# Two activation functions, one table or two: how ScalarE is told which table to hold

## The reference

```python
for i in range(2):                       # first block; ctx is a second stream of 256 rows
    hx = rms_norm(x, g_mix[i]) * (1 + sc1) + sh1
    zx = hx @ w_in[i]                    # q, k, v, a pooling part, a Fourier part
    q = apply_rope(head_rms(zx_q, q_gain[i])); k = apply_rope(head_rms(zx_k, k_gain[i]))
    x = x + ga1 * (concat(attention, pool_mix, fourier_mix) @ w_out[i])
    fx = rms_norm(x, g_ffn[i]) * (1 + sc2) + sh2
    x = x + ga2 * swiglu(fx, w_gate_up[i], w_down[i])    # the same for ctx where i == 0
proj = modulate(x, norm1_g) @ w_in_2     # second block: attention, mLSTM, mixture of experts
attn = head_rms_norm(moba_attention(...)); hm = head_rms_norm(mlstm_chunkwise(...)) * sigmoid(o_m)
x = x + g1 * (concat(attn, hm) @ w_out_2)
x = x + g2 * hier_moe(modulate(x, norm2_g))              # 32 experts, every weight is read
return rms_norm(x, norm_f_g)
```

## Time and profile before

| what | value |
|---|---|
| time, median of 3 runs | 1589.12 us (1587.69 to 1589.77) |
| the profiled execution's own time | 1589.12 us |
| its span in the profile | 1587.3 us |
| TensorE busy | 1388.9 us, 88% |
| VectorE busy | 714.0 us, 45% |
| ScalarE busy | 500.9 us, 32% |
| GpSimd busy | 59.2 us, 4% |
| mean granted TensorE clock | 0.936 |
| read from HBM | 392.32 MB |

### The profile page before, as it was taken

How to read it: one execution, slowest core, us unless ns; L and a number is a source line. 1 busy time by engine, 2 the same in 40 slices (tenths; PEclk the granted TensorE clock), 3 DMA queues, 4 the chain that set the end, 5 groups by cost and what they waited for, 6 DMA issues and landing times.

```text
span 1587.3 us, 24627 instructions
## 1 busy us (share of the span) xinstructions
PE 1388.9 (88%) x10276; PEld 1042.8 (66%) x10276; DVE 714.0 (45%) x1306; ACT 500.9 (32%) x952; POOL 59.2 (4%) x52
## 2 busy tenths in 40 slices
PE   6999999999999999978999999999896677667564
PEld 3754576877778776847999989898653333333232
DVE  4446445555555564565655667676521111110101
ACT  3426424222122223454543444554310000000001
POOL 0100022000000012101000000000000000000000
PEclk8999999999999999999999999999997787887877
DMA  9637354645754563806456428245899999999996
GB/s 361 263 137 247 100 208 176 226 156 202 263 185 175 185 212 107 231 7 238 131 181 204 128 76 293 81 134 212 343 424 422 423 425 423 424 424 424 423 425 259
DMA packets 172651, 395.03 MB, mean 249 GB/s; under 512 B 11620, under 2 KB 124792, under 8 KB 150776
## 3 DMA queue, kind: packets, MB, share of 16 engines
q1 hardware_dynamic: 171816, 391.91, 66.4%
q10 hardware_dynamic: 720, 1.49, 0.2%
HBM read 392.32 MB, written 1.05 MB: 248 GB/s over the span
## 4 chain that ended last, share of the span: by engine, by line
PE 68%; DMA 22%; DVE 4%; ACT 3%; issue 2%; SPq 1%; POOL 0%; DVEq 0%; ACTq 0%; POOLq 0%
DMA R<-in_w_dram 20%; PE ps L985 15%; PE ps L986 15%; PE ps L991 15%; PE ps L2839 3%; PE ps L1007 2%; PE ps L1008 2%; PE ps L1013 2%; DMA R<-in_w_ada_dram 1%; PE ps L2888 1%; PE ps L1301 1%; PE ps L1358 1%; PE ps L2917 1%; PE ps L630 1%; PE ps L1332 1%
## 5 line engine op out<-in xcount | busy, mean ns | idle before, releaser
L954 DVE TENSOR_TENSOR WL<-R,WH 128x1024 fp32r<-128x1024 f32 (+1 forms) x202 | 225.3, 1128 | 140.1 <-ACT WH L944 140.0
L2839 PE MATMUL ps<-R,XG 128*32 128x256 f32 x2048 | 174.2, 501 | 119.2 <-DMA R<-in_w_dram 113.2
L985 PE MATMUL ps<-HH,WH 128*128 128x256 f32 (+2 forms) x872 | 274.3, 334 | 0.0
L986 PE MATMUL ps<-HL,WH 128*128 128x256 f32 (+2 forms) x872 | 270.8, 332 | 0.0
L944 ACT ACTIVATE WH<-R 128x1024 fp32r<-128x1024 f32 (+1 forms) x202 | 191.1, 961 | 156.3 <-PE ps L991 120.1
L2839 PEld LDWEIGHTS ps<-R,XG 128*32 128x32 f32 x2048 | 86.5, 138 | 200.7 <-issue 184.7
L985 PEld LDWEIGHTS ps<-HH,WH 128*128 128x128 f32 (+1 forms) x872 | 165.4, 190 | 24.6 <-issue 3.6
L986 PEld LDWEIGHTS ps<-HL,WH 128*128 128x128 f32 (+1 forms) x872 | 164.7, 189 | 16.3
L991 PE MATMUL ps<-HH,WL 128*128 128x256 f32 (+2 forms) x872 | 165.0, 331 | 0.0
L985 PE MATMUL ps<-GH,WH 128*128 128x512 f32 (+1 forms) x480 | 154.1, 340 | 0.0
L986 PE MATMUL ps<-GL,WH 128*128 128x512 f32 (+1 forms) x480 | 153.4, 338 | 0.0
(11 more groups left out here) (480 smaller groups left out, 1736.4 us busy)
## 6 DMA issues: line engine op xcount, KB each, us to landing
R<-in_w_dram SPq DMA_DIRECT2D x192, 1024.0 KB, 22.5
R<-in_w_ada_dram SPq DMA_DIRECT2D x72, 1024.0 KB, 6.9
R<-in_w_gate_up_dram SPq DMA_DIRECT2D x40, 1024.0 KB, 7.7
R<-in_w_in_dram SPq DMA_DIRECT2D x20, 1024.0 KB, 8.8
R<-in_w_down_dram SPq DMA_DIRECT2D x16, 768.0 KB, 4.5
R<-in_w_down_dram SPq DMA_DIRECT2D x16, 640.0 KB, 4.4
R<-in_w_in_dram SPq DMA_DIRECT2D x8, 512.0 KB, 7.2
R<-in_w_out_dram SPq DMA_DIRECT2D x16, 256.0 KB, 8.6
```

The source lines that it names most:

```text
L954: last = e.tensor_tensor(L, w, H.bitcast(F32), ALU.subtract)
L985: e.matmul(b[0:n, 0:N], H[:, k, 0:n], xh(k, N), start=(k == 0), stop=False)
L986: e.matmul(b[0:n, 0:N], H[:, k, 0:n], xl(k, N), start=False, stop=False)
L2839: mm = e.matmul(PS[4][32 * g:32 * g + 32, 0:256], x[:, 4 * hf + k, :], w[g // 2][:, k, 256 * (g % 2):256 * (g % 2) + 256], start=(hf == 0 ...
```

## The change

The requests for a table by name go away. In `act_rstd` a small activation of one column (`act_warm`: Ln of a constant, its result used by nobody) stands in their place, and in the second block two of the requests go with nothing in their place; the one for Sqrt becomes a one-column Sqrt. A new semaphore `s_warm` orders these small activations among themselves; its waits are for earlier instructions of the same engine.

```diff
-    LN_EXP = "natural_log_exp_and_others"
-
-    def act_rstd(e, n, N):
-        e.preload_act_table_set(LN_EXP)
+    def act_warm(e, w):
+
+        if w:
+            e.wait_ge(s_warm, w)
+        e.activation(EB[:, 1:2], ONES[:, 0:1], ACT.Ln).then_inc(s_warm, 1)
+
+    def act_rstd(e, n, N, w):
+        act_warm(e, w)
         e.wait_ge(s_sum, 8 + 3 * n)
...
         elif j == 25:
             act_silu2(e, 3)
-            e.preload_act_table_set(LN_EXP)
             act_head_squares(e, 0)
...
             e.activation(OM[:, :, :], OM[:, :, :], ACT.Sigmoid).then_inc(s_mla, 1)
-            e.preload_act_table_set(LN_EXP)
...
             if j == 3:
-                e.preload_act_table(ACT.Sqrt)
+                e.wait_ge(s_warm, 5)
+                e.activation(EB[:, 1:2], ONES[:, 0:1], ACT.Sqrt).then_inc(s_warm, 1)
```

More of the change, by code:

```diff
@@ L320, in block_program @@
     s_fd, s_fp, s_fq, s_r5, s_root = (sem(n) for n in ("s_fd", "s_fp", "s_fq", "s_r5", "s_root"))
-    s_cvt, s_wd = sem("s_cvt"), sem("s_wd")
+    s_cvt, s_warm, s_wd = sem("s_cvt"), sem("s_warm"), sem("s_wd")
     s_kq, s_hbc, s_hpk = sem("s_kq"), sem("s_hbc"), sem("s_hpk")
@@ L1737, in act_layer @@
             act_split(e, t0 + 1)
-            act_rstd(e, 2, 512)
+            act_rstd(e, 2, 512, 2)
         else:
@@ L1763, in act_layer @@
         act_split(e, t1 + 1)
-        act_rstd(e, 2 * i + 1, N)
+        act_rstd(e, 2 * i + 1, N, 2 * i + 1)
         act_norm(e, 2 * i + 1, N, i == 0, 256, lambda k: MOD[:, i, 24 + k, 0:1])
@@ L2383, in act_second @@
         e.dma_start(TWO[:, :], A["k_two"]).then_inc(d_two2, 16)
-        act_rstd(e, 4, 256)
+        act_rstd(e, 4, 256, 4)
         act_norm(e, 4, 256, False, 256, lambda k: MOD[:, 2, k, V2:V2 + 1])
@@ L3146, in _ @@
             act_square(e, 0, 5, 512)
-            act_rstd(e, 0, 512)
+            act_rstd(e, 0, 512, 0)
             act_layer(e, 0)
```

## The result

| | before | after |
|---|---|---|
| median of the runs shown together | 1588.51 us (1583.69 to 1589.77) | 1598.88 us (1597.83 to 1599.11) |
| ratio, 95% interval | | 1.0063 (1.0048 to 1.0079) |
| the profiled execution's own time | 1589.12 us | 1598.26 us |
| its span | 1587.3 us | 1596.5 us |
| ScalarE busy | 500.9 us | 523.5 us |

The changed kernel is slower by 0.63%. Between the two profiled executions it is 9.1 us, between the medians 10.4 us, and the interval of the ratio is 7.6 to 12.5 us. 1600.2 us had been forecast. The record has ten runs of the changed kernel, from 1594.14 to 1599.11 us with their median at 1598.35 us; the five of the table lie in the upper part of that.

What follows compares the result with a forecast made beforehand. TensorE was taken to bound the kernel up to about 1115 us, transfers from 1170 us on. The profiled 1589.12 us plus 9.38 of path and 1.7 of clock gave 1600.2 us, range 1595.5 to 1604.0 us.

Steps and rivals of the forecast that it cites:

- 9.38 us of path: Sum of forecast TensorE delays: norms 1 and 2, norms 3 and 4, layer 1 head norms, gates, last head norms.
- One load, 1.283 us and 0.02 us around it: On ScalarE, each added table load between close instructions costs 1.29 us; norms 1 and 2 together cost 2.58 us.
- The dearer switch: Rival: a load between Ln and Exp costs twice its length, 10.2 us more in all, 1610.4 us; chance 0.04.
- Norms 3 and 4, 2 x 1.49: At each of these norms, a one-column Ln of up to 0.20 us plus a load of 1.29 us; 2.98 us together.
- Head norms of layer 1, 1.26: Two loads each at keys and queries delay weight copies and VectorE's scaling, so TensorE's spreading of roots comes 1.26 us later.
- Gates, 1.28: A load before the gates' Ln delays a weight copy and the whole VectorE chain to the scores' exponential: 1.28 us.
- Last head norms, 1.28: Second block: two loads around the Ln delay rounding and scaling, so TensorE's transposes start 1.28 us later.
- The places at nothing: Norm 0, layer 0 head norms, first scores' Exp, second block's first head norms and the Sqrt: cost 0.
- The clock, +1.7: Longer TensorE stops at norms 1 and 2 bring a slow stretch behind at least one: +1.7 us, between 0 and +3.4.
- the likeliest case: Of none, one or two extra slow clock stretches (1598.5, 1600.2 or 1601.9 us), one was held likeliest.
- Not slower, because the experts' transfers take it in: Rival at 1113 to 1170 us: the weight stream starts independently of TensorE, so the end stays at 1589.1 us; chance 0.04.

Runs made afterwards that it cites:

- the kernel with the inner loads behind the waits: Kernel before plus the changed kernel's loads at layer 1 head norms (requested after the waits), gates and last head norms only: 1594.02 us, ratio 1.0045.
- the one with the loads costed at nothing: Kernel before plus eight loads at norm 0, layer 0 head norms, first scores' Exp and second block's first head norms: 1590.20 us, one run.

## Why the prediction was right

The forecast was 1600.2 us, the median 1598.9 us; 9.38 us of path had been summed, and the steps of the table, less the clock, are 9.0.

- **One load, 1.283 us and 0.02 us around it.** Right: 1.28 at norms 1 and 2 (1.29 forecast), and linear in the number of loads. The dearer switch is refuted, and with it, for this chip and this kernel, the drain of about 1380 ns that the Trainium skill adds in "ScalarE: Activation LUTs", section "What ACT_TABLE_LOAD costs"; its 1283 ns agree with all 34 loads. Where they differ the measurement decides.
- **Norms 3 and 4, 2 x 1.49.** The stops grew by 1.37 and 1.38. The one-column Ln had been put at up to 0.20, its busy time, and costs 0.10, the distance to the start of the Ln behind it: 0.2 us too much in the sum.
- **Head norms of layer 1, 1.26.** Right in size, 1.22, and nearly in its way: of this, 0.51 came behind the keys. There TensorE waited for the roots themselves, 0.43 us, and not for the copy behind them as I had it:

```profile
661.04 1.09 PE L1158 MATMUL ps<-RSK,HPK 32*128 32x512 f32 x2 [0.43 <-ACT RSK L1142]
...
670.64 0.36 PE L989 MATMUL ps<-HH,WH 128*128 128x256 f32 x1 [0.34 <-ACT WH L948]
```

- **Gates, 1.28.** Right: 1.27. The chain through VectorE has no slack.
- **Last head norms, 1.28.** The size was right, 1.22, the path was not: the place is TensorE's wait for the split at 1098.21, which this matmul did not have in before, and not the transposes, which I had delayed by the scaling of the heads:

```profile
1098.21 0.39 PE L1011 MATMUL ps<-M2H,WH 128*128 128x256 f32 x1 [1.17 <-DVE M2L L2085]
```

- **The places at nothing.** Right: no step at them that the kernel before doesn't show between its own two profiles.
- **The clock, +1.7.** The mechanism was right and its net size was not. One slow stretch did follow norm 1, and none norm 2, as the likeliest case had it. It cost 2.81 - 1.28 = 1.53 us. That it was one and not two is in part luck: stops of the same 2.89 us were followed by two in the kernel with one load in each norm. Norms 3 and 4 brought 0.06 and 0.49 more. But the profiled execution also came to norm 1 ahead of the one of before, by 1.66 us. The first matmul behind norm 0 was 0.71 us ahead already, here of before and then of the changed kernel:

```profile
37.78 0.79 PE L1007 MATMUL ps<-HH,WH 128*128 128x512 f32 x1 [2.81 <-DVE HL L829]
```

```profile
37.07 0.80 PE L1011 MATMUL ps<-HH,WH 128*128 128x512 f32 x1 [2.80 <-DVE HL L833]
```

Ahead of it TensorE had waited 2.1 us for the first weights in place of 3.0. The other 0.9 us came behind it, where the first slow time ended at 40.5 us in place of 43.1 (it was 10.2 us long where that of before was 13.7). Nothing shows that either comes from the change: the kernel with loads only in the experts' stage had 10.2 us of slow time there too, and the second profile of the changed kernel, with the same 10.2, came to norm 1 only 0.58 us ahead. So the profile shows the path's 9.0, the clock's +2.1 and the start's -1.7, and 9.35 in all; the medians show 10.4.

- **Not slower, because the experts' transfers take it in.** Refuted by the equal 460 us windows. The experiment in that stage shows how near it was: a delay of that size, and three times it, costs nothing when it falls behind the start of the stream.

The experts' stage began 9.45 us late, and I had written about 11; the difference is mostly the start again.

## What to carry to other kernels

Ask for the table that holds both functions, by name, where a function pair alternates; in this kernel each was otherwise given its own, and every alternation cost 1.28 us where what followed was on TensorE's path and ScalarE had no wait of that length. Put a request ahead of the wait of the activation it serves, anywhere behind the last activation that needs another table: then it lies in the wait. Cost a load by the place and not by the sum: of 17 added, ten made up the 9 us and seven cost nothing.

## What the runs showed of the chip that I had not expected

- A longer stop of TensorE makes a slow stretch likelier, not certain. Behind the stops of 1.6 to 1.7 us at norms 1 and 2, 16 in the eight profiles with no load added there, the granted clock never fell. Behind those of 2.9 to 4.2 us, eight in four profiles, it fell to 0.50 for 3.4 us in six. Each cost 1.3 to 1.6 us. The length of a stop alone doesn't decide: one of 1.51 us in the second block, at 1083 us in before, is in all twelve profiles, and a slow stretch came within a microsecond of its end in ten.
- A slow stretch can also follow a stop of 1.0 or 1.4 us where no other profile has one: twice, in the kernel with the inner loads behind the waits and in the one with the loads costed at nothing.
- TensorE's slow time at the start was 6.8, 10.2 or 13.7 us in different executions, 13.7 in both of the kernel before. With the waits for the first weights it moves everything behind it, by 1.7 us between the two profiles compared at first: almost a fifth of the effect to be explained.
- In the experts' stage the granted clock was higher, 0.88 for 0.81, in the execution with more waits for VectorE and fewer for transfers. Over the whole program, the mean granted clock of its ten runs was 0.955 to 0.961, that of the kernel before on the same chip 0.935 to 0.945. Why is open.
